# Six places of a hand-ordered layer kernel: state copies ahead of a gate, weights ahead of halves, turns and sums later, most of the last norm's sums earlier

## The chip, the cores and the metric

One core of a Trainium2 chip. The metric is device microseconds for one launch, the median of several runs. Names of engines: PE is TensorE's matmul, PEld its weight load (which overlaps matmuls), DVE is VectorE, ACT ScalarE, POOL GpSimd, SP the queue that issues loads.

## The reference, cut to what matters

One layer of a hybrid decoder at width 1024, for 320 tokens (256 of a prompt, 8 sequences of 8 tokens that continue old states), in float32:

```
x = x + 0.5 * g1 * swiglu(modulate(rmsnorm(x)))            # ff1
mq, mk, mv, mo, mi, mf, z, xbc, dtp, ga, gb = split(u @ w_in)
hm = mlstm(conv(mq, mk), mv, gates, C, n, m)               # 4 heads, 256 x 512 states
ya = (headnorm(hm) * sigmoid(mo)) @ w_pa
ys = ssd(conv(xbc), dt, A, h) + D * xs                     # 32 heads in 4 groups
gg = ys * silu(z)
gg = gg * rsqrt(mean(gg * gg over a group's 512) + EPS)    # group norm
yb = (gg * s_norm_g) @ w_pb
x = x + g2 * ((sigmoid(ga) * ya + sigmoid(gb) * yb) @ w_out)
x = x + 0.5 * g3 * swiglu(modulate(rmsnorm(x)))            # ff2
y = rmsnorm(x, final_norm)
```

## The kernel before

Activations lie transposed, 128 channels by 320 tokens a tile. Every product with a weight is cut into **units**: one unit gives one output tile of 128 channels from 8 weight tiles. Float32 accuracy comes from three products of halves: `dense` issues eight matmuls w_hi by u_hi, eight w_hi by u_lo, eight w_lo by u_hi, all into one of the banks of PSUM. ScalarE makes the high half of a unit's weights from the loaded ring (`high_ahead`, tile w_hi), VectorE the low half (`low_ahead`, tile w_lo), both two units ahead; the high half of the unit after next waits until the present unit is done, since there are two buffers.

Each engine has its own program, written by hand as loops over the same list of units; between the units it does the small work of that stage. What an engine does after which unit is given by `if i == ...` and by tables, so the order on each engine is fixed, and semaphores join them. The stages that matter here, in order:

- **The four mLSTM heads**, units v and mo. The last head has eight mo units (i = 0 to 7). `turn_head` transposes one of four 128-channel parts of a head's normalised output back; `TURN_SLOTS` says behind which unit. ScalarE normalises a head (`output_norm`, `hn_ready`); it gates with mo (`output_gate`), VectorE multiplies (`gated_head`) and splits.
- **pa**, then the first xbc units.
- **Four groups of the SSD** (`gr` 0 to 3), eight units each (`phase_units`). In the first three the fifth unit (i = 4) is an xbc unit, in the last it is a z unit. TensorE issues behind unit i: `decay_rows` (i < 4), `pack_inputs` (i = 2, waits for `hmask_ready`), `head_outputs(gr, i - 1)` (i = 1 to 4, waits for `w_ready`), in this order; `turn_states` and `sample_states` from i = 4. VectorE: `sample_masks` makes sample halves and masks (b_halves, x_halves, cm, `hmask_ready`) and the decays' rows; `weights` multiplies decays by scores (`w_ready`); `outputs` adds D * x. ScalarE: `old_states` copies turned states (`ht_read`), `gate` applies the gate's function to a bank.
- **Twelve tail units**: z 12 to 15, ga 4 to 7, gb 4 to 7 (i = 0 to 11). ScalarE squares a group's tiles, POOL adds the four tiles, TensorE sums over channels with one-column matmuls (`group_sums`, tile aux<-ones), ScalarE takes the roots of three groups at once (`roots(0, 3)`), VectorE their reciprocals (`group_roots` there, `rr_ready`), TensorE broadcasts them over partitions (`group_roots` there, aux<-ident,sm, behind unit i = 4), and VectorE scales the tiles (`group_norm`).
- **pb, out, ff2, the last norm**: seven tiles' squares are added by POOL while the eighth is computed; one-column matmuls sum both, then root, reciprocal, scaling and the store of y.

ScalarE's functions come in table sets; a change of set is an ACT_TABLE_LOAD in the profile. Copy and Square need no load of their own here.

Of the kernel before, what the change touches and what calls it, by code (L numbers as in the profile page):

```python
# [14 lines left out]
KD = D // 128  # L15
# [41 lines left out]
STEP_SLOTS = (1, 2, 4, 5)  # L57
TURN_SLOTS = ({}, {3: 0, 4: 1, 5: 2}, {0: 3, 3: 4, 4: 5, 5: 6}, {0: 7, 3: 8, 4: 9, 5: 10, 6: 11})
EARLY = {name: [(name, 0), (name, 1)] for name in ("qk", "up2")}
# [188 lines left out]
def build(nc, io, out):  # L248
# [5 lines left out]
    with ctx:  # L254
# [749 lines left out]
        def _(pe):  # L1004
# [805 lines left out]
            for i, u in enumerate(tail_units()):  # L1810
                dense(u)
                if i == 0:
                    turn_old_part(SG - 1)
                    pe.wait_ge(S["up_done"], 16)
                    turn_tails(4, 6, (banks[2], banks[3]))
                if i == 2:
                    group_sums(0)
                if i == 3:
                    group_sums(1)
                    group_sums(2)  # L1820
                if i == 4:
                    for gr in range(3):
                        group_roots(gr)
                if i == 6:
                    group_sums(3)
# [33 lines left out]
            pe.wait_ge(S["sq_summed"], 4 + SG)  # L1859
            pe.wait_ge(S["sq_ready"], 4 * KD)  # L1860
            for c in range(3):
                rows = 128 if c < 2 else 64
                t = slice(c * 128, c * 128 + rows)
                mm(aux[3][0:rows, c:c + 1], sq[:, 0, t], ones[:, 0:1], True, False)
                ins = mm(aux[3][0:rows, c:c + 1], sq[:, KD - 1, t], ones[:, 0:1], False, True)
            ins.then_inc(S["rowsum_done"], 1)
# [4 lines left out]
        def _(act):  # L1871
# [517 lines left out]
            for gr in range(SG):  # L2389
                us = phase_units(gr)  # L2390
                for i, u in enumerate(us):
                    if i >= 5:
                        old_states(gr, i - 4)
                    high_ahead(u)
                    if u.name == "xbc":
                        conv(u, pad2, 3)
                    elif u.name == "gb":
                        if u.own == 0:
                            act.wait_ge(S["conv_silu"], 40)
                        kept_gate(u, ACT.Copy)  # L2400
                    else:
                        gate(u, ACT.Copy if i < 4 else gate_func(u))
# [21 lines left out]
                    if i == 5:  # L2424
                        act.wait_ge(S["ph_mm"], gr + 1)
                        copy(prompt_h, aux[2][:, :]).then_inc(S["ph_copied"], 1)
                    if i == 4:
                        old_states(gr, 0)
# [28 lines left out]
            for i, u in enumerate(tail_units()):  # L2457
# [9 lines left out]
                if i == 1:  # L2467
                    squares(2)
                if i == 3:
                    roots(0, 3)  # L2470
                if i == 4:
                    squares(3)
                    nc.scalar.activation(merged_g[:, 0:4, :], merged_g[:, 0:4, :], ACT.Sigmoid).then_inc(S["gate_open"], 1)
                    for r in range(4):
                        act.wait_ge(state_out[r], 16 * old_uses[r] + 32 * SG)
                    act.wait_ge(prompt_sent, 16 * (MH + SG))
# [52 lines left out]
        def _(dve):  # L2529
# [722 lines left out]
            for gr in range(SG):  # L3252
                for i, u in enumerate(phase_units(gr)):
# [12 lines left out]
                    if i == 0:  # L3266
                        group_rows(gr)
                        masked_scores(gr)
                    if i == 1:
                        if gr > 0:  # L3270
                            old_part(gr - 1)
                        sample_masks(gr)
                    if i < 4 and not amid:
                        weights(gr, i)
                    if 1 <= i <= 3 and not amid:
                        outputs(gr, i - 1)
                    if i == 4:
                        weighted_inputs(gr)
# [27 lines left out]
            for i, u in enumerate(tail_units()):  # L3306
# [3 lines left out]
                if u.name != "gb":  # L3310
                    gated(u, ya if u.name == "ga" else xbc_t)
                if i == 3:
                    group_roots(0, 3)
# [93 lines left out]
```

## Time and profile before

| | |
|---|---|
| median of 3 runs | 1263.19 us (1263.02 to 1265.1) |
| profiled execution | 1262.8 us |
| its span, first to last instruction | 1261.1 us |
| mean granted TensorE clock | 0.993 |
| PE busy | 1240.4 us, 98% |
| PEld busy | 1144.7 us, 91% |
| DVE, ACT, POOL busy | 783.3, 620.8, 220.8 us |
| HBM | 190 GB/s over the span |

The span is what the trace covers; the profiled execution's own time is 1.7 us more. A busy PE is not PE at its peak, since the ends of matmuls are modelled; idle TensorE shows in the timelines as a bracket behind a row, with the length of the idle time and what ended it. The table's shares are averages over all stages; the places of the change are looked at one by one below.

### The profile page before, as it was taken

To read this page: it belongs to the slowest core of one execution; us is meant where nothing else is said; L and a number is where in the kernel's file an instruction comes from. 1 tells how busy PE (TensorE), PEld (TensorE's weight loads), DVE (VectorE), ACT (ScalarE), POOL (GpSimd) and SP (SyncE) were. 2 spreads that over 40 slices of the span, in tenths; PEclk is the share of its full clock that TensorE was granted. 3 is DMA by queue.
4 is the path that set the end of the run, shared out by engine and by line. 5 is a ranking of instruction groups with operands and counts; after the bars stand their busy time and mean duration, and the time that the engine had idled before them with its cause. 6 is when DMAs were issued, how large, how long until landed. Compare 5 with 4: busy or idle time off the path is not lost. (4 is left out here: it accounts for less than half of the span.)

```text
span 1261.1 us, 22606 instructions
## 1 busy us (share of the span) xinstructions
PE 1240.4 (98%) x9059; PEld 1144.7 (91%) x9059; DVE 783.3 (62%) x1345; ACT 620.8 (49%) x1102; POOL 220.8 (18%) x385
## 2 busy tenths in 40 slices
PE   8999999999999999999999999999999999999997
PEld 5999989998988777779999989989999999999997
DVE  4744444547976667675388787875676885455432
ACT  5523324335668555655356776565543453333432
POOL 5100000012640212130033333414200300000000
PEclk8999999999999999999999999999999999999998
DMA  9998879553324788986474558365454454653541
GB/s 310 264 345 261 260 252 300 158 167 127 117 85 145 254 299 306 355 272 173 140 206 129 158 153 243 105 206 155 127 138 152 152 190 145 200 160 111 161 138 42
DMA packets 258629, 241.54 MB, mean 192 GB/s; under 512 B 8205, under 2 KB 242141, under 8 KB 258526
## 3 DMA queue, kind: packets, MB, share of 16 engines
q1 hardware_dynamic: 249850, 211.16, 54.6%
q0 software_dynamic: 8576, 28.91, 6.8%
q8 instruction: 72, 1.18, 0.4%
q14 instruction: 31, 0.25, 0.1%
q10 hardware_dynamic: 100, 0.04, 0.0%
HBM read 209.88 MB, written 30.21 MB: 190 GB/s over the span
## 5 line engine op out<-in xcount | busy, mean ns | idle before, releaser
L2552 DVE TENSOR_TENSOR w_lo<-ring,w_hi 128x1024 fp32r<-128x1024 f32 (+1 forms) x264 | 337.6, 1279 | 354.4 <-ACT w_hi L1889 353.8
L1889 ACT ACTIVATE w_hi<-ring 128x1024 fp32r<-128x1024 f32 (+1 forms) x264 | 289.6, 1097 | 485.7 <-PE bank L1010 441.7
L1010 PE MATMUL bank<-u_hi,w_hi 128*128 128x320 f32 x1472 | 257.5, 316 | 0.7 <-ACT w_hi L1889 0.5
L1010 PE MATMUL bank<-u_hi,w_lo 128*128 128x320 f32 x1472 | 247.0, 310 | 0.4 <-DVE w_lo L2552 0.4
L1010 PE MATMUL bank<-u_lo,w_hi 128*128 128x320 f32 x1472 | 246.4, 310 | 0.0
L1010 PEld LDWEIGHTS bank<-u_hi,w_hi 128*128 128x128 f32 x1472 | 222.8, 188 | 16.3 <-issue 9.6
L1010 PEld LDWEIGHTS bank<-u_hi,w_lo 128*128 128x128 f32 x1472 | 223.7, 188 | 1.3 <-DVE w_lo L2552 1.2
L1010 PEld LDWEIGHTS bank<-u_lo,w_hi 128*128 128x128 f32 x1472 | 224.3, 188 | 0.1
L818 POOL TENSOR_TENSOR arena<-x_t,gain 128x64 f32<-128x64 f32 x16 | 4.8, 298 | 337.4 <-DVE x_t L2634 337.4
L1010 PE MATMUL bank<-ff_hi,w_hi 128*128 128x320 f32 x352 | 57.5, 310 | 0.0
L1010 PE MATMUL bank<-ff_hi,w_lo 128*128 128x320 f32 x352 | 56.8, 308 | 0.0
L1010 PE MATMUL bank<-ff_lo,w_hi 128*128 128x320 f32 x352 | 56.8, 308 | 0.0
L1010 PEld LDWEIGHTS bank<-ff_hi,w_hi 128*128 128x128 f32 x352 | 52.7, 188 | 0.4 <-issue 0.4
L1010 PEld LDWEIGHTS bank<-ff_hi,w_lo 128*128 128x128 f32 x352 | 52.9, 188 | 0.0
L1010 PEld LDWEIGHTS bank<-ff_lo,w_hi 128*128 128x128 f32 x352 | 52.9, 188 | 0.0
L1007 PE MATMUL aux<-ident,arena 128*128 128x128 f32 (+4 forms) x325 | 49.7, 278 | 3.0 <-ACT arena L1875 1.6
L790 POOL TENSOR_TENSOR arena<-arena 128x320 f32<-128x320 f32 x12 | 10.4, 868 | 226.0 <-ACT arena L1908 225.2
L2822 DVE SCALAR_TENSOR_TENSOR arena<-arena,par 128x344 f32<-128x344 f32 x80 | 46.7, 584 | 3.9 <-POOL arena L858 1.8
L1010 PE MATMUL bank<-y_hi,w_hi 128*128 128x320 f32 x272 | 45.9, 310 | 0.0
L1007 PEld LDWEIGHTS aux<-ident,arena 128*128 128x128 f32 (+4 forms) x325 | 37.2, 141 | 9.5 <-issue 4.3
L1010 PE MATMUL bank<-y_hi,w_lo 128*128 128x320 f32 x272 | 45.8, 310 | 0.0
L1010 PE MATMUL bank<-y_lo,w_hi 128*128 128x320 f32 x272 | 45.7, 309 | 0.0
(426 smaller groups left out, 1682.1 us busy)
## 6 DMA issues: line engine op xcount, KB each, us to landing
ring<-in_w_in SPq DMA_DIRECT2D x52, 1024.0 KB, 5.4
ring<-in_ff_w SPq DMA_DIRECT2D x44, 1024.0 KB, 7.5
ring<-in_ff_w SPq DMA_DIRECT2D x32, 704.0 KB, 4.7
arena<-in_ada_w SPq DMA_DIRECT2D x20, 1024.0 KB, 10.0
ring<-in_ada_w SPq DMA_DIRECT2D x16, 1024.0 KB, 11.9
arena<-in_state_mlstm_C SPq DMA_DIRECT2D x22, 512.0 KB, 6.6
out_s_C<-arena POOLq DMA_DIRECT2D x22, 512.0 KB, 6.9
ring<-in_w_pa SPq DMA_DIRECT2D x8, 1024.0 KB, 8.0
```

The lines of the kernel that those rows point to most:

```text
L790: ins = nc.gpsimd.tensor_tensor(sq[:, 0, :], sq[:, 0, :], sq[:, kc, :], ALU.add)
L818: nc.gpsimd.tensor_tensor(sequences(xg_s[n][:, kc, :]), sequences(x_t[:, kc, TP:T]), gain[:, kc, 1:NSEQ].unsqueeze(2).to_broadcast([128, S ...
L1007: return nc.tensor.transpose(dst, src, ident[0:rows, 0:rows])
L1010: return nc.tensor.matmul(dst, lhs, rhs, start=first, stop=last)
L1889: nc.scalar.activation(w_hi[v.split_no % 2][:, 0:v.kc, :], panel_part(v), ACT.Copy).then_inc(S["hi_done"], 1)
L2552: V.tensor_tensor(w_lo[r][:, 0:v.kc, :], panel_part(v), w_hi[r][:, 0:v.kc, :].bitcast(FP32), ALU.subtract)\
L2822: ch.link(V.scalar_tensor_tensor(out=a, in0=p[:, tap:tap + CONVW], scalar=par[:, c + w_col + tap * tiles:c + w_col + tap * tiles + 1], in1 ...
```

## The change

Six edits of order; no arithmetic is changed, and no instruction added or removed but for one table load on ScalarE.

1. ScalarE, last group: the copies of the first turned states stand ahead of the fifth unit's gate, not behind.
2. VectorE, every group, behind the second unit: `weights` and `outputs` stand ahead of `sample_masks`.
3. Last head: four of its five turns move one slot later (3, 4, 5, 6 to 4, 5, 6, 7). The table is read by TensorE, ScalarE (`gated_high`) and VectorE (`gated_head`, `gated_low`).
4. TensorE, tail: the third group's sums move from behind the fourth unit into the fifth, between its first and second eight matmuls.
5. ScalarE and VectorE, tail: the roots of three groups and their reciprocals move from behind the fourth unit's gate to behind the fifth's. TensorE's broadcasts of them stay behind the fifth unit.
6. TensorE, last norm: for each block of tokens the sum over seven tiles and the eighth's square stood together, behind the wait for the latter; now the three of the seven tiles come first, then the wait, then the three of the eighth. Only the first of the six starts an accumulation.

```diff
--- before.py
+++ after.py
@@ -55,7 +55,7 @@
 PA_ORDER = (0, 2, 4, 6, 1, 3, 5, 7) + tuple(range(8, 16))
 PART_ORDER = (0, 2, 4, 1, 3, 5) + tuple(range(6, 16))
 STEP_SLOTS = (1, 2, 4, 5)
-TURN_SLOTS = ({}, {3: 0, 4: 1, 5: 2}, {0: 3, 3: 4, 4: 5, 5: 6}, {0: 7, 3: 8, 4: 9, 5: 10, 6: 11})
+TURN_SLOTS = ({}, {3: 0, 4: 1, 5: 2}, {0: 3, 3: 4, 4: 5, 5: 6}, {0: 7, 4: 8, 5: 9, 6: 10, 7: 11})
 EARLY = {name: [(name, 0), (name, 1)] for name in ("qk", "up2")}
 CONV_AT = {0: (), 1: (), 2: (0,), 3: (1,), 4: (2,), 5: (3, 4), 6: (5,), 7: (6, 7)}
 XBC_FIRST = tuple(range(16, 24)) + tuple(range(4))
@@ -1808,7 +1808,7 @@
 
             pe.wait_ge(S["tails_saved"], 40)
             for i, u in enumerate(tail_units()):
-                dense(u)
+                dense(u, inner=(lambda: group_sums(2)) if i == 4 else None)
                 if i == 0:
                     turn_old_part(SG - 1)
                     pe.wait_ge(S["up_done"], 16)
@@ -1817,7 +1817,6 @@
                     group_sums(0)
                 if i == 3:
                     group_sums(1)
-                    group_sums(2)
                 if i == 4:
                     for gr in range(3):
                         group_roots(gr)
@@ -1857,12 +1856,13 @@
                 if u.closes and u.own > 0:
                     turn_result(u.own - 1)
             pe.wait_ge(S["sq_summed"], 4 + SG)
-            pe.wait_ge(S["sq_ready"], 4 * KD)
-            for c in range(3):
-                rows = 128 if c < 2 else 64
-                t = slice(c * 128, c * 128 + rows)
-                mm(aux[3][0:rows, c:c + 1], sq[:, 0, t], ones[:, 0:1], True, False)
-                ins = mm(aux[3][0:rows, c:c + 1], sq[:, KD - 1, t], ones[:, 0:1], False, True)
+            for kc in (0, KD - 1):
+                if kc > 0:
+                    pe.wait_ge(S["sq_ready"], 4 * KD)
+                for c in (0, 2, 1):
+                    rows = 128 if c < 2 else 64
+                    t = slice(c * 128, c * 128 + rows)
+                    ins = mm(aux[3][0:rows, c:c + 1], sq[:, kc, t], ones[:, 0:1], kc == 0 and c == 0, kc > 0 and c == 1)
             ins.then_inc(S["rowsum_done"], 1)
             turn_result(KD - 1)
 
@@ -2392,6 +2392,8 @@
                     if i >= 5:
                         old_states(gr, i - 4)
                     high_ahead(u)
+                    if i == 4 and u.name != "xbc":
+                        old_states(gr, 0)
                     if u.name == "xbc":
                         conv(u, pad2, 3)
                     elif u.name == "gb":
@@ -2424,7 +2426,7 @@
                     if i == 5:
                         act.wait_ge(S["ph_mm"], gr + 1)
                         copy(prompt_h, aux[2][:, :]).then_inc(S["ph_copied"], 1)
-                    if i == 4:
+                    if i == 4 and u.name == "xbc":
                         old_states(gr, 0)
                     if i == 7:
                         old_part(gr)
@@ -2466,9 +2468,8 @@
                     squares(1)
                 if i == 1:
                     squares(2)
-                if i == 3:
+                if i == 4:
                     roots(0, 3)
-                if i == 4:
                     squares(3)
                     nc.scalar.activation(merged_g[:, 0:4, :], merged_g[:, 0:4, :], ACT.Sigmoid).then_inc(S["gate_open"], 1)
                     for r in range(4):
@@ -3266,14 +3267,14 @@
                     if i == 0:
                         group_rows(gr)
                         masked_scores(gr)
-                    if i == 1:
-                        if gr > 0:
-                            old_part(gr - 1)
-                        sample_masks(gr)
+                    if i == 1 and gr > 0:
+                        old_part(gr - 1)
                     if i < 4 and not amid:
                         weights(gr, i)
                     if 1 <= i <= 3 and not amid:
                         outputs(gr, i - 1)
+                    if i == 1:
+                        sample_masks(gr)
                     if i == 4:
                         weighted_inputs(gr)
                         if u.name == "xbc":
@@ -3309,7 +3310,7 @@
                     old_part(SG - 1)
                 if u.name != "gb":
                     gated(u, ya if u.name == "ga" else xbc_t)
-                if i == 3:
+                if i == 4:
                     group_roots(0, 3)
                 if 4 <= i <= 9:
                     for c in range(2 * (i - 4), 2 * (i - 4) + 2):
```

How this moves instructions, at three places. First ScalarE in the tail, from the copy behind the fourth unit on; arena<-bank is a gate, sm<-aux,eps_col the roots of the three groups, w_hi<-ring a high half, arena<-arena 128x1280 a square (and, last, the sigmoid of the merge gates). Before:

```order
L1889 ACTIVATE w_hi<-ring 128x1024
L2314 ACTIVATE arena<-bank 128x320
L2449 ACT_TABLE_LOAD
L2449 ACTIVATE sm<-aux,eps_col 128x2x3
L2450 ACTIVATE sm<-aux,eps_col 64x3
L1889 ACTIVATE w_hi<-ring 128x1024
L2314 ACT_TABLE_LOAD
L2314 ACTIVATE arena<-bank 128x320
L2443 ACTIVATE arena<-arena 128x1280
L2473 ACTIVATE arena<-arena 128x1280
```

The same place in the changed kernel (its lines are two further on):

```order
L1889 ACTIVATE w_hi<-ring 128x1024
L2314 ACTIVATE arena<-bank 128x320
L1889 ACTIVATE w_hi<-ring 128x1024
L2314 ACT_TABLE_LOAD
L2314 ACTIVATE arena<-bank 128x320
L2451 ACT_TABLE_LOAD
L2451 ACTIVATE sm<-aux,eps_col 128x2x3
L2452 ACTIVATE sm<-aux,eps_col 64x3
L2445 ACTIVATE arena<-arena 128x1280
L2474 ACT_TABLE_LOAD
L2474 ACTIVATE arena<-arena 128x1280
```

The roots moved behind the next unit's high half, table load and gate, and a further table load stands ahead of the last sigmoid.

TensorE at the same place: the one-column sums of the second and third group (two rows each), and the unit around them; the broadcasts follow the unit's last eight matmuls in both kernels.

```order
 L1010 MATMUL aux<-ones,arena 128x1 x2
 L1010 MATMUL aux<-ones,arena 64x1
+L1010 MATMUL bank<-u_hi,w_hi 128x320 x8
 L1010 MATMUL aux<-ones,arena 128x1 x2
 L1010 MATMUL aux<-ones,arena 64x1
-L1010 MATMUL bank<-u_hi,w_hi 128x320 x8
 L1010 MATMUL bank<-u_lo,w_hi 128x320 x8
 L1010 MATMUL bank<-u_hi,w_lo 128x320 x8
```

The first eight matmuls of the unit moved ahead of the third group's sums.

VectorE in a group, behind the second unit: weights is the 128x896 row, outputs the 128x320 row, the four rows from b_halves on are `sample_masks`. Before:

```order
L3249 TENSOR_TENSOR arena<-arena 128x2x4x32
L3187 TENSOR_TENSOR b_halves<-arena,b_halves 64x128
L3188 TENSOR_TENSOR x_halves<-arena,x_halves 64x512
L3190 TENSOR_TENSOR arena<-arena,seg_b 128x128 x2
L3195 TENSOR_TENSOR w_lo_rest<-sm,tile_of_head 32x256
L3216 SCALAR_TENSOR_TENSOR arena<-arena 128x896
L3221 SCALAR_TENSOR_TENSOR arena<-arena,h_dec,bank 128x320
```

And in the changed kernel (its lines are one further on):

```order
L3250 TENSOR_TENSOR arena<-arena 128x2x4x32
L3217 SCALAR_TENSOR_TENSOR arena<-arena 128x896
L3222 SCALAR_TENSOR_TENSOR arena<-arena,h_dec,bank 128x320
L3188 TENSOR_TENSOR b_halves<-arena,b_halves 64x128
L3189 TENSOR_TENSOR x_halves<-arena,x_halves 64x512
L3191 TENSOR_TENSOR arena<-arena,seg_b 128x128 x2
L3196 TENSOR_TENSOR w_lo_rest<-sm,tile_of_head 32x256
```

Weights and outputs moved ahead of the halves, the masks and the decays' rows.

## Rows read from the trace of the kernel before

**Rows 1.** The page: busy time, share and instructions of each engine.

```profile
PE 1240.4 (98%) x9059; PEld 1144.7 (91%) x9059; DVE 783.3 (62%) x1345; ACT 620.8 (49%) x1102; POOL 220.8 (18%) x385
```

**Rows 2.** Windows: stretch, length, PE busy, granted clock, DMA share, GB/s.

```profile
11.70:18.50 6.80, 6.80 (x44) 0.50 1.10 350
...
888.90:892.30 3.40, 3.40 (x15) 0.50 0.76 216
```

**Rows 3.** Timelines: start, us, engine, line; PE in two groups, ACT in the last.

```profile
749.42 0.66 PE L1010 MATMUL bank<-pack_b,pack_x 32*128 32x128 f32 x8
750.02 1.09 PE L1007 MATMUL aux<-ident,arena 128*128 128x128 f32 x8
...
848.76 0.66 PE L1010 MATMUL bank<-pack_b,pack_x 32*128 32x128 f32 x8
850.43 1.06 PE L1007 MATMUL aux<-ident,arena 128*128 128x128 f32 x8 [1.01 <-ACT arena L1875]
...
848.06 1.28 ACT L2314 ACT_TABLE_LOAD   x1
```

**Rows 4.** Timelines of ACT, DVE and PEld, second group, second and third unit.

```profile
733.30 0.35 ACT L2371 ACTIVATE arena<-aux,g 128x64 f32<-128x64 f32 x1
...
733.30 0.42 DVE L3249 TENSOR_TENSOR arena<-arena 128x256 f32<-128x256 f32 x1
734.23 0.28 DVE L3187 TENSOR_TENSOR b_halves<-arena,b_halves 64x128 fp32r<-64x128 f32 x1 [0.51 <-ACT x_halves L1875]
...
735.15 0.49 DVE L3190 TENSOR_TENSOR arena<-arena,seg_b 128x128 f32<-128x128 f32 x2
...
735.89 1.07 DVE L3216 SCALAR_TENSOR_TENSOR arena<-arena 128x896 f32<-128x896 f32 x1
736.89 0.53 DVE L3221 SCALAR_TENSOR_TENSOR arena<-arena,h_dec,bank 128x320 f32<-128x320 f32 x1
...
735.87 0.39 PEld L1010 LDWEIGHTS aux<-x_halves,pick_x 128*128 128x128 f32 x2
737.02 0.63 PEld L1010 LDWEIGHTS bank<-arena 128*64 128x64 f32 x8 [0.75 <-DVE arena L3216]
```

**Rows 5.** Timelines of PEld, ACT and PE around the last head.

```profile
545.93 0.31 PEld L1007 LDWEIGHTS bank<-ident,arena 128*128 128x128 f32 x3 [0.94 <-ACT arena L2265]
...
573.44 0.80 ACT L2265 ACTIVATE arena<-arena,coef 64x512 f32<-64x512 f32 x1
...
575.24 1.47 PE L1007 MATMUL aux<-ident,arena 128*128 128x128 f32 x12
```

**Rows 6.** Timelines of PEld, ACT and DVE in the tail units.

```profile
887.40 0.73 PEld L1010 LDWEIGHTS aux<-ones,arena 128*128 128x128 f32 x6 [0.82 <-POOL arena L986]
888.15 1.47 PEld L1010 LDWEIGHTS bank<-u_hi,w_hi 128*128 128x128 f32 x8
...
893.16 2.98 PEld L1010 LDWEIGHTS aux<-ident,sm 128*128 128x128 f32 x18
896.20 1.17 PEld L1010 LDWEIGHTS bank<-u_hi,w_hi 128*128 128x128 f32 x8
...
888.92 0.27 ACT L2449 ACTIVATE sm<-aux,eps_col 128x6 f32<-128x6 f32 x1
...
893.56 1.06 ACT L1889 ACTIVATE w_hi<-ring 128x1024 fp32r<-128x1024 f32 x1 [4.23 <-PE bank L1010]
894.64 1.28 ACT L2314 ACT_TABLE_LOAD   x1
895.93 0.44 ACT L2314 ACTIVATE arena<-bank 128x320 f32<-128x320 f32 x1
...
889.47 0.12 DVE L3294 RECIPROCAL sm<-sm 64x3 f32<-64x3 f32 x1
```

**Rows 7.** Timeline of PE at the end of the program.

```profile
1252.29 1.35 PE L1010 MATMUL aux<-ones,arena 128*128 128x1 f32 x12 [1.30 <-ACT arena L1908]
1253.57 0.55 PE L1007 MATMUL aux<-ident,arena 128*128 128x128 f32 x3
```

## The prediction

> **What bounds the kernel now.** The page first: TensorE is busy for 1240.4 of 1261.1 us [rows 1], and no other engine for more than 62%. So only time in which TensorE waits, or runs slowly, can be won or lost, and whatever it loses lasts to the end. The timelines of its matmuls (PE) and weight loads (PEld) show where it stands still at the places that the diff touches; there the other engines' timelines say what ends last. The windows show where its clock is not at full: two stretches only, 6.8 us at the start and 3.4 us from 888.9, both at half rate, 1.2 of 2.4 GHz [rows 2]. Between the waits a unit of 24 matmuls takes 3 x 1.17 = 3.5 us [rows 6].
>
> **State copies ahead of the gate (a gain of 1.05).** The edit acts in the last group alone, whose fifth unit is a z unit. Now ScalarE loads a table (1.28) and copies the gate before the two state copies, and TensorE's turns of the next states wait 1.01 for them: from the packed products to these turns it is 1.67 us, against 0.60 in the second group, where no table load stands there [rows 3]. With the copies first, nothing new is waited for: 1.67 - 0.60 = 1.07, taken as 1.05. The gate comes some 1.1 us later; the bank that it frees is opened two units on, over 7 us away, so I cost that at nothing. Without the cover it would be 1.1.
>
> **Weights ahead of halves (a loss of 0.7, four places).** In a group's second unit VectorE makes the sample halves and masks (from 734.23), then the rows for the grown decays, then weights (735.89, 1.07), and TensorE waits 0.75 for these [rows 4]. It looks like a gain of 0.5: the packing's two matmuls of 512 columns stream for 0.43 at 2.4 GHz behind a load of some 0.2, so to about 736.5, and from there to 737.02 nothing streams. But TensorE's own order is inputs packed, then outputs, and packing needs the masks, which now come last. After: the weights can start when VectorE's addition ends, 733.30 + 0.42 = 733.72, and ScalarE's last exponential is done (733.65); with 0.03 for the start, 733.75. Weights to outputs take 1.00, the outputs 0.53 less the same overlap of 0.07, halves to masks 0.92, the masks 0.49: done at 736.62, seen by TensorE at 736.68 (weights ended at 736.96 and TensorE went on at 737.02). The packing that started at 735.87 now waits 0.81, and behind it lie its 0.43, with or without the 0.2: outputs start at 737.1 to 737.3, against 737.02 [rows 4]. That is +0.1 to +0.3 a group; I take nearly 0.2, so 0.7, with 0.3 to 1.2 for the four. The first group lacks the addition but has the same order and nearly the same waits.
>
> **A head's turns one slot later (a gain of 0.9).** The turn in slot 3 of the last head waits 0.94 for the normalised rows [rows 5]. One slot later they are long there. The turn itself moves behind the last mo unit and costs the same there. Late next could be the last head's own rows: they are ready at 573.44 + 0.80 = 574.24 and asked for at 575.24 [rows 5], 1.0 of slack. TensorE comes 0.9 sooner, and ScalarE too, less one gated copy that now lies ahead (about 0.4): some 0.5 of slack is left, and if it is used up the gain shrinks by as much. Bounds: 0.94 and 0.5.
>
> **Last norm's sums ahead (a gain of 0.65).** Twelve passes of one column take 1253.57 - 1252.29 = 1.28, behind a wait of 1.30 for the last square, and everything behind them waits [rows 7]. Six go into that wait. Half of 1.28 is 0.64. Bounds: 0.5 and 0.7.
>
> **A group's sums later, and the roots.** Three terms.
> The wait for the third group's sums, 0.82 [rows 6], goes: eight matmuls of the next unit (1.17) now lie ahead of them. -0.8.
> Behind it stands the low clock. That unit takes 893.16 - 888.15 = 5.01 instead of 3.51, since from 888.9 the granted clock is 0.50 [rows 2, 6]. Ahead of the fall there were twelve one-column passes and the wait; with 1.2 us of dense matmuls between them and no wait I expect no fall. -1.5.
> But the square roots now come behind the fifth unit's gate on ScalarE, and the gate needs the fifth unit finished; TensorE's broadcasts of the roots still stand right behind that unit, and wait for them. Now that unit covers the roots; the cover goes. The chain, from the unit's last load (893.16 now): 0.40 to the copy of high halves, 2.37 from there to the gate (1.06 copy, 1.29 table load), 0.44 gate, 1.29 for a second table load, 0.67 from the first root to the end of the reciprocals (888.92 to 889.47 + 0.12), 0.05 to be seen. Sum 5.22 [rows 6]. TensorE has nothing else queued ahead of the broadcasts: +5.2. VectorE's normalisation of tiles stands behind the reciprocals; its results are first needed by pb, seven units on.
> The clock falls in such a wait, by what a far shorter one did [rows 2]. The 18 broadcast passes then run slower: 0.166 each now, while twelve turns of 128 columns take 0.12 each at full rate [rows 5], so 0.24 at half, and 18 x 0.075 = 1.3 at most. What is left of the slow stretch lies on dense matmuls. Bounds: nothing, and 1.3 + 1.5 with dense matmuls slowed as at 888.9. I take 0.8, since much of such a stretch passes in the wait itself.
> The three and the clock: -0.8 - 1.5 + 5.2 + 0.8 = +3.7. The further table load that the sigmoid of the merge gates now needs (1.28) lies under the next unit.
>
> A rule speaks against this even more. The Trainium skill, ScalarE: Activation LUTs, section What ACT_TABLE_LOAD costs, puts 1.38 us of drain beside the 1.28 of each switch. This trace disagrees: the high copy ends at 894.62 and the load begins at 894.64, and the gate begins as the load ends [rows 6]. By the page the chain would be longer by 2 x 1.38, and the sum +4.5.
>
> **Sum.** -1.05 + 0.7 - 0.9 - 0.65 + 3.7 = +1.8. The profiled execution took 1262.8 (span 1261.1 and 1.7 around it), the median is 1263.19; both shift alike: 1265.0 us. It is 0.14%, and a measurement of this kernel tells 0.2% (2.5 us) from no change: under 1260.7 is faster, over 1265.7 slower.
>
> **The rivals.**
> As summed: the wait for the roots eats the gains. Adding the bounds that are likely together gives 1263.6 to 1266.9. 0.63.
> The clock stays low longer, as in the 6.8 us at the start [rows 2], slower. Place: behind the roots' wait. Price: 4.3 us of slowed broadcasts (+1.3) and 2.5 of dense matmuls at half rate (+1.2), 2.5 instead of 0.8: 1266.7. It decides once the slow clock costs over 1.5 there (0.8, and the 0.7 up to 1265.7). For it: such a stretch exists, with light work in it; against: the later one lasted only 3.4. 0.16. The Trainium skill, TensorE: Matmul & The Clock Gate, Part 1, says that the default of the array's clock is throttled and activity releases it. The trace agrees in so far as both stretches began in light work and ended in activity; between their lengths no row decides.
> The weights do win: if packing were not waited for, 4 x 0.5 = 2.0 is gained instead of 0.7 lost: 1262.3, no change. For it: the wait is named for the weights. Against: packing needs the masks, and the sum of VectorE's work ahead of it grows by 1.46. 0.08.
> The roots' wait is not what it seems, and the change is faster: if the broadcasts found the roots ready, 5.2 + 0.8 would go: 1259.0. For it: everything else in the change gains. Against: their chain starts at the end of the very unit that they follow. 0.06.
> Table loads with their drain: by a wait longer by 2.8 us, 1267.8. Against it, the rows' gap of 0.02. 0.07.
>
> **How the numbers follow.** 1265.0 is the likeliest case's. Its own range, 1263.6 to 1266.9, widened towards both neighbours until 2 in 10 is out, is 1262.3 to 1267.4. Slower: 0.16 + 0.07 and the upper sixth of the first case, 0.12, is 0.35. Faster: 0.06, and 0.02 of the third. Same: 0.57.
>
> **What would show it.** In the profile after: the broadcasts of the roots (aux<-ident,sm) preceded by some 5 us of idle TensorE, and a granted clock of 0.50 there; no idle before the third group's sums, and a full clock in the unit around them; the packing (x_halves,pick_x) waiting 0.8 in each group for masks, and the outputs behind it for nothing; no wait before the turns of states in the last group, nor before the last head's first late turn; six one-column passes before the last square, six after. If the wait for the roots is under 3 us, the forecast is wrong and the kernel faster; if the outputs in the groups start earlier than now, the second step is wrong.

## The result and the profile after

The changed kernel takes 1273.6 us (median of 4 runs, 1272.98 to 1273.89) against 1263.51 beside it: ratio 1.0077, interval 1.006 to 1.0094. It is slower by 10.1 us, where 1.8 was forecast, and lies above the range. Its profiled execution took 1272.98 us, with a span of 1270.0 against 1261.1.

The page's first part after; it answers to [rows 1]. PE's busy time has grown by 5.0 us though no matmul was added. Not all of that is the change's: up to a row of the last head just ahead of the first edit's place (540.27 before, 540.83 after) PE is busy 534.05 us against 531.86, and stands still 1.6 less. From there to the end it is busy 2.8 us more and stands still 5.5 more.

```profile
PE 1245.4 (98%) x9059; PEld 1147.1 (90%) x9059; DVE 783.7 (62%) x1345; ACT 622.7 (49%) x1103; POOL 217.4 (17%) x385
```

**A new wait at the last head.** First the timeline of PEld after, from the last rows of the last head into pa; then ACT's and DVE's of the same stretch (start, us, engine and line; in the bracket the idle time before and what ended it). They answer to [rows 5].

```profile
573.18 1.18 PEld L1010 LDWEIGHTS bank<-y_hi,w_hi 128*128 128x128 f32 x8 [1.89 <-issue]
...
578.31 1.29 PEld L1007 LDWEIGHTS aux<-ident,arena 128*128 128x128 f32 x12 [1.61 <-ACT arena L2265]
```

```profile
568.13 0.59 ACT L1875 ACTIVATE arena<-bank 64x512 f32<-64x512 f32 x1 [4.99 <-PE bank L1007]
...
572.67 0.44 ACT L2188 ACTIVATE arena<-bank 128x320 f32<-128x320 f32 x1 [1.95 <-DVE w_lo_rest L3040]
...
577.46 0.80 ACT L2265 ACTIVATE arena<-arena,coef 64x512 f32<-64x512 f32 x1
```

```profile
568.76 0.68 DVE L3049 TENSOR_TENSOR arena<-bank,arena 64x512 f32<-64x512 f32 x1 [4.62 <-ACT arena L1875]
...
571.92 0.17 DVE L3061 TENSOR_SCALAR coef<-coef 128x3 f32<-128x3 f32 x1
572.03 0.55 DVE L3040 SCALAR_TENSOR_TENSOR w_lo_rest<-bank,par,arena 128x320 f32<-128x320 f32 x1
```

The wait of 0.94 in slot 3 is gone, but two waits, 1.89 and 1.61, have come. Read them backwards. pa's second unit starts 0.07 after ScalarE's gate (572.67 + 0.44) frees its bank. The gate waited 1.95 for VectorE's product with the twelfth turn (572.03), and that product stands behind the statistics of the last head's rows (568.76 to 572.09). These began late since ScalarE stood idle for 4.99 us ahead of the copy of those rows (568.13), until a TensorE transposition had been done. In the code that copy is `output_rows(3)`, which overwrites the tile nm that the turns read, so it waits until all twelve turns are done (`hn_turned`), and the twelfth now comes behind the last mo unit. Before, the same copy waited for nothing; ACT's row:

```profile
563.80 0.59 ACT L1875 ACTIVATE arena<-bank 64x512 f32<-64x512 f32 x1
```

The norm of the rows, which ended at 574.24 before, ends at 578.26, and the turns of pa wait for it.

**The packing waits for the masks.** The timelines of PEld and DVE in the second group; they answer to [rows 4].

```profile
740.38 0.30 PEld L1010 LDWEIGHTS aux<-x_halves,pick_x 128*128 128x128 f32 x2 [0.95 <-DVE arena L3191]
741.04 0.63 PEld L1010 LDWEIGHTS bank<-arena 128*64 128x64 f32 x8 [0.37 <-issue]
```

```profile
738.34 0.54 DVE L3222 SCALAR_TENSOR_TENSOR arena<-arena,h_dec,bank 128x320 f32<-128x320 f32 x1
738.91 0.28 DVE L3188 TENSOR_TENSOR b_halves<-arena,b_halves 64x128 fp32r<-64x128 f32 x1
...
739.83 0.49 DVE L3191 TENSOR_TENSOR arena<-arena,seg_b 128x128 f32<-128x128 f32 x2
```

The packing waits 0.95 for VectorE's masks, and the outputs start 0.66 behind it: 1.61 where before it was 737.02 - 735.87 = 1.15 [rows 4]. That is +0.46 in this group. By the same two rows it is 0.44, 0.47 and 0.47 in the other three, 1.8 in all.

**The roots.** PEld in the tail, then ACT, then the windows with the granted clock (stretch, length, busy times, clock, DMA share, GB/s); they answer to [rows 6] and [rows 2].

```profile
893.53 1.22 PEld L1010 LDWEIGHTS bank<-u_hi,w_lo 128*128 128x128 f32 x8
899.96 0.74 PEld L1010 LDWEIGHTS aux<-ident,sm 128*128 128x128 f32 x4 [5.21 <-DVE sm L3295]
...
905.07 2.05 PEld L1010 LDWEIGHTS bank<-u_hi,w_hi 128*128 128x128 f32 x8
...
909.41 1.22 PEld L1010 LDWEIGHTS bank<-u_hi,w_hi 128*128 128x128 f32 x8
```

```profile
895.11 1.06 ACT L1889 ACTIVATE w_hi<-ring 128x1024 fp32r<-128x1024 f32 x1 [3.61 <-PE bank L1010]
896.18 1.28 ACT L2314 ACT_TABLE_LOAD   x1
897.48 0.44 ACT L2314 ACTIVATE arena<-bank 128x320 f32<-128x320 f32 x1
897.93 1.28 ACT L2451 ACT_TABLE_LOAD   x1
899.23 0.27 ACT L2451 ACTIVATE sm<-aux,eps_col 128x6 f32<-128x6 f32 x1
```

```profile
888.50:900.20 11.70, 6.76 (x49) 6.43 (x48) 5.60 (x8) 6.41 (x9) 2.67 (x2) 1.00 0.44 127
900.20:907.00 6.80, 6.80 (x25) 5.77 (x25) 1.01 (x2) 3.15 (x3) 2.39 (x2) 0.50 0.00 0
```

The wait is the forecast one, 5.21. The clock is full all through it and falls to 1.2 GHz only 0.2 us after work has begun again. So the whole slow stretch lies on work: the 18 broadcasts take 905.07 - 899.96 = 5.11 against 3.04, the next unit 909.41 - 905.07 = 4.34 against 3.48: 2.9 us.

The other steps went as forecast. The sums of the third group wait for nothing, and the unit around them runs at full clock. In the last group the turns of the next states come 0.59 behind the packed products, against 1.67 [rows 3]; PE after:

```profile
853.70 0.66 PE L1010 MATMUL bank<-pack_b,pack_x 32*128 32x128 f32 x8
854.29 1.09 PE L1007 MATMUL aux<-ident,arena 128*128 128x128 f32 x8
```

PEld at the end of the program, which answers to [rows 7]:

```profile
1260.11 0.36 PEld L1007 LDWEIGHTS aux<-ident,arena 128*128 128x128 f32 x3
1260.47 0.82 PEld L1010 LDWEIGHTS aux<-ones,arena 128*128 128x128 f32 x6
1261.95 0.81 PEld L1010 LDWEIGHTS aux<-ones,arena 128*128 128x128 f32 x6 [0.66 <-ACT arena L1908]
1262.60 0.37 PEld L1007 LDWEIGHTS aux<-ident,arena 128*128 128x128 f32 x3
```

And the same two turns before:

```profile
1250.35 0.37 PEld L1007 LDWEIGHTS aux<-ident,arena 128*128 128x128 f32 x3
...
1253.56 0.28 PEld L1007 LDWEIGHTS aux<-ident,arena 128*128 128x128 f32 x3
```

From one turn to the next it is 2.49 after and was 3.21 before, a gain of 0.72.

### The profile page after: what moved, and what is told of

Read it like the earlier page. It is cut to its first block and busy times, and to the rows that moved or that the text cites. A ratio compares the mean times of both kernels' runs of the same rounds, so it can differ in the third digit from the quotient of the medians.

```text
span 1270.0 us, 22609 instructions
## 1 busy us (share of the span) xinstructions
PE 1245.4 (98%) x9059; PEld 1147.1 (90%) x9059; DVE 783.7 (62%) x1345; ACT 622.7 (49%) x1103; POOL 217.4 (17%) x385
## 5 line engine op out<-in xcount | busy, mean ns | idle before, releaser
L790 POOL TENSOR_TENSOR arena<-arena 128x320 f32<-128x320 f32 x12 | 10.4, 867 | 226.5 <-ACT arena L1908 225.2
```

Of the source, the lines that this page charges most:

```text
L790: ins = nc.gpsimd.tensor_tensor(sq[:, 0, :], sq[:, 0, :], sq[:, kc, :], ALU.add)
```

## The experiments

All are made from the kernel before. The start of the program varies by some 4 us between executions of any of these kernels, so beside the medians I give a distance inside each profiled execution: from a row of TensorE in the last head (aux<-vp,kpm x2 with an idle time of 0.84, at 540.27 before) to the turn behind the last norm's sums (1253.57 before, the last row of [rows 7]). It leaves the start out, but it is one execution of each kernel and has no interval. A last column says whether the clock fell in or behind the third group's sums, ahead of the broadcasts, as it did before ([rows 2], worth 1.5).

| kernel | median us | before beside it | ratio and interval | distance, us | less before's | fall at the sums |
|---|---|---|---|---|---|---|
| before | 1263.19 | | | 713.30 | | yes |
| after | 1273.6 | 1263.51 | 1.0077 [1.006, 1.0094] | 721.88 | +8.6 | no |
| roots_only | 1273.2 | 1264.0 | 1.0076 [1.006, 1.0092] | 720.68 | +7.4 | no |
| turns_only | 1266.51 | 1264.0 | 1.002 [1.0011, 1.0029] | 716.02 | +2.7 | yes |
| masks_only | 1265.64 | 1264.0 | 1.0016 [1.0006, 1.0026] | 715.11 | +1.8 | yes |
| copies_and_last_sums | 1262.59 | 1264.0 | 0.9989 [0.9978, 1.0] | 710.26 | -3.0 | no |
| last_turn_only | 1268.39 | 1263.67 | 1.004 [1.0026, 1.0054] | 716.84 | +3.5 | yes |
| turns_two | 1262.22 | 1263.67 | 0.9992 [0.9982, 1.0001] | 711.00 | -2.3 | no |
| sums_in_unit_roots_kept | 1262.69 | 1263.67 | 0.9991 [0.9982, 1.0] | 711.11 | -2.2 | no |
| roots_before_gate | 1268.6 | 1263.67 | 1.0043 [1.0029, 1.0056] | 719.08 | +5.8 | no |
| roots_only_spun | 1267.04 | 1263.26 | 1.0023 [1.0014, 1.0033] | 716.18 | +2.9 | no |
| weights_then_masks | 1263.19 | 1263.26 | 1.0003 [0.9994, 1.0012] | 711.84 | -1.5 | no |
| masks_split | 1262.24 | 1263.26 | 0.9991 [0.9981, 1.0] | 711.94 | -1.4 | yes |
| best | 1257.1 | 1263.26 | 0.9949 [0.9936, 0.9962] | 707.05 | -6.3 | no |

### Parts of the change, alone

**roots_only**: the third group's sums into the fifth unit, and roots and reciprocals behind its gate (edits 4 and 5).

```diff
-                dense(u)
+                dense(u, inner=(lambda: group_sums(2)) if i == 4 else None)
...
-                if i == 3:
+                if i == 4:
                     roots(0, 3)
```

> Only the third group's sums move into the fifth tail unit and the roots behind its gate. Theory: a wait of 5.2 us before the broadcasts, and behind it a stretch of 6.8 us at half clock that lies wholly on work, +2.9 us; less the 2.3 gained before, +5.9 us. Rival, as predicted: +3.7 us, half clock costing 0.8.

**turns_only**: edit 3 alone.

```diff
-TURN_SLOTS = (..., {0: 7, 3: 8, 4: 9, 5: 10, 6: 11})
+TURN_SLOTS = (..., {0: 7, 4: 8, 5: 9, 6: 10, 7: 11})
```

> Only the last head's turns move one slot later. Theory: ScalarE's copy of the last head's numerators waits until the twelfth turn has been issued (it overwrites the rows that the turns read); that turn now stands behind the last mo unit, so the copy, the statistics and the norm come some 4 us later and TensorE waits for them in pa, 1.9 and 1.6 us: +2.6 us in all, after the 0.9 gained in slot 3. Rival, the step as I predicted it: -0.9 us, and the 3.5 lost in pa come from another part of the change.

**masks_only**: edit 2 alone, `sample_masks` behind weights and outputs.

```diff
-                        sample_masks(gr)
                     if i < 4 and not amid:
                         weights(gr, i)
                     if 1 <= i <= 3 and not amid:
                         outputs(gr, i - 1)
+                    if i == 1:
+                        sample_masks(gr)
```

> Only VectorE's weights and outputs move ahead of halves and masks. Theory: +0.45 us in each of four groups, +1.8 us: the packing waits 0.9 for the masks, and the outputs behind it start 0.66 after the packing does. Rival, as predicted: +0.7 us, the packing waiting 0.8 and the outputs following after 0.43 to 0.63.

**copies_and_last_sums**: edits 1 and 6.

```diff
+                    if i == 4 and u.name != "xbc":
+                        old_states(gr, 0)
...
+            for kc in (0, KD - 1):
+                if kc > 0:
+                    pe.wait_ge(S["sq_ready"], 4 * KD)
```

> Only the state copies ahead of the last group's gate, and the last norm's sums of seven tiles ahead of the eighth's square. As predicted: -1.05 - 0.65 = -1.7 us, 1261.5. If the four parts add up (2.6 + 1.8 + 5.9 - 1.7 = 8.6), no part acts on another. Rival: the sum of the four differs from the whole by over 1 us, and parts act on each other.

Measured: the roots are the largest loss, and turns and masks lose as well. The last two edits gain; of their 3.0, 1.5 is the fall of the clock that did not come in this execution. The four medians add up to 9.2 + 2.5 + 1.6 - 1.4 = 11.9 against 10.1 for the whole. In the distances, without the 1.5, they give 7.4 + 2.7 + 1.8 - 1.5 = 10.4 against 8.6. Of these 1.8, 1.4 are explained: in roots_only's execution the slow stretch was longer. The other 0.4 is left open. PEld of roots_only, and the windows:

```profile
900.23 0.93 PEld L1010 LDWEIGHTS aux<-ident,sm 128*128 128x128 f32 x4 [5.21 <-DVE sm L3292]
...
905.53 2.10 PEld L1010 LDWEIGHTS bank<-u_hi,w_hi 128*128 128x128 f32 x8
...
911.07 1.22 PEld L1010 LDWEIGHTS bank<-u_hi,w_hi 128*128 128x128 f32 x8
```

```profile
900.30:910.30 10.00, 10.00 (x36) 8.97 (x37) 1.00 (x2) 3.32 (x3) 2.40 (x2) 0.51 0.00 0
```

The same wait of 5.21, then 5.30 for the broadcasts and 5.54 for the unit, 4.3 us more than at full clock (2.26 and 2.06), where it was 2.9 after.

### Which turn does the harm

**last_turn_only**: only the twelfth turn moves, from slot 6 to 7.

```diff
+TURN_SLOTS = (..., {0: 7, 3: 8, 4: 9, 5: 10, 7: 11})
```

> Only the twelfth turn moves, from slot 6 to slot 7 of the last head; turns 8 to 10 stand as before. Theory (ScalarE's copy of the last head's rows waits for the twelfth turn, and holds the high copy and the gate behind it): TensorE waits some 1.9 us ahead of pa's second unit and some 1.6 us ahead of the turns of pa, as where all four turns are late, and the wait of 0.94 us in slot 3 is back too: +3.5 us of TensorE time around the last head, about 1266.7. Rival (what hurts is that all four turns lie one slot later, so that each delays ScalarE's chain a little): the two waits are under 1 us together, and the time is within 0.5 us of before.

**turns_two**: the other three move one slot, and the twelfth shares slot 6 with the eleventh.

```diff
+TURN_SLOTS = (..., {0: 7, 4: 8, 5: 9, 6: 10})
...
+                        turn_head(2, 3)
...
+                        gated_high(11)
```

> Turns 8, 9 and 10 one slot later (slots 4, 5 and 6), but the twelfth turn stays in slot 6, behind the eleventh; nothing stands behind the last mo unit. Theory (the twelfth turn's place behind the last mo unit is the whole harm): the wait of 0.94 us in slot 3 is gone, the waits of 1.9 and 1.6 us of the changed kernel are gone, and TensorE gains 0.9 us: about 1262.5. Rival (a later place for any turn delays the last head's rows): waits of over 0.5 us stay ahead of the turns of pa, and nothing is gained.

Timeline of PEld, last_turn_only:

```profile
546.74 0.31 PEld L1007 LDWEIGHTS bank<-ident,arena 128*128 128x128 f32 x3 [0.94 <-ACT arena L2265]
...
574.32 1.19 PEld L1010 LDWEIGHTS bank<-y_hi,w_hi 128*128 128x128 f32 x8 [1.89 <-issue]
...
579.45 1.29 PEld L1007 LDWEIGHTS aux<-ident,arena 128*128 128x128 f32 x12 [1.59 <-ACT arena L2265]
```

And PEld, then ACT, of turns_two:

```profile
576.13 1.38 PEld L1007 LDWEIGHTS aux<-ident,arena 128*128 128x128 f32 x12
```

```profile
565.99 0.59 ACT L1876 ACTIVATE arena<-bank 64x512 f32<-64x512 f32 x1 [1.47 <-PE bank L1007]
...
574.48 0.80 ACT L2266 ACTIVATE arena<-arena,coef 64x512 f32<-64x512 f32 x1
```

The twelfth turn alone brings both waits, and the old 0.94 with them: the distance is 3.5 longer, as the theory says. The median moved by 4.7, 1.2 more than the distance, and why is open. With it in slot 6 the copy of the last head's rows waits 1.47, the norm ends at 575.28, and nothing waits. The distance is 2.3 shorter, 1.5 of it the absent fall and 0.9 the wait that is gone. By medians the gain can't be told from none.

### The roots: wait and clock apart

**sums_in_unit_roots_kept**: edit 4 without edit 5.

```diff
+                dense(u, inner=(lambda: group_sums(2)) if i == 4 else None)
```

> The third group's sums inside the fifth tail unit, while ScalarE's roots stay behind the fourth unit's gate. Theory (the loss of this part is the roots' place alone): no wait of 0.82 us ahead of the sums; the broadcasts of the roots wait for nothing; the clock stays full from 885 to 910 us: -0.8, and a further -1.5 where the kernel before has its slow clock there: 1261.2 to 1262.7. Rival (sums later make the roots late as well): the roots wait for the sums, whose end is now 1.2 us later, and the broadcasts wait 0.5 to 1.5 us: no gain.

**roots_before_gate**: behind the fifth unit's high half but ahead of its gate; the reciprocals ahead of the product with the gate.

```diff
+                if i == 4:
+                    roots(0, 3)
...
-                if i == 3:
-                    roots(0, 3)
```

> The third group's sums inside the fifth tail unit; the roots behind ScalarE's high half of the fifth unit but ahead of its gate, the reciprocals ahead of VectorE's product with the gate. Theory (the broadcasts wait for the chain on ScalarE behind the fifth unit): high copy, table load, roots, reciprocals remain, the gate and its table load fall out: the wait is 3.4 us instead of 5.2, and a slow stretch of the clock still follows; +2.6 for the wait less the 0.8 of the sums and up to 2.9 for the clock: 1266 to 1270. Rival (what slows TensorE is the broadcasts' own work of narrow passes, not the wait): the slow stretch is as long as with the wait of 5.2 us.

**roots_only_spun**: as roots_only, with 22 products of the identity with itself ahead of the broadcasts; the result goes to a bank that nobody reads.

```diff
+                    pe.wait_ge(S["tail_cp"], 2)
+                    spin(22)
```

> As with the roots behind the fifth unit's gate, but TensorE multiplies the identity by itself 22 times ahead of the broadcasts (work that computes nothing and whose result nobody reads), so that it is busy in the time in which it waits for the roots. Theory (the roots' chain costs 5.2 us, and the idle wait itself brings the slow clock, which costs 2.9 us and more behind it): the broadcasts start as late as without the added work, the granted clock stays full, they take 3.0 us and the next unit 3.5: 2.9 to 4 us less than the kernel with the roots moved alone, about 1269.5. Rival (the slow clock comes from the narrow passes of the broadcasts): the clock falls there as before and nothing is won; also if the added work lasts past the roots, the broadcasts come later by that.

PEld of sums_in_unit_roots_kept, then of roots_before_gate, then of roots_only_spun:

```profile
889.16 0.76 PEld L1010 LDWEIGHTS aux<-ones,arena 128*128 128x128 f32 x6
...
892.24 2.98 PEld L1010 LDWEIGHTS aux<-ident,sm 128*128 128x128 f32 x18
```

```profile
895.84 0.93 PEld L1010 LDWEIGHTS aux<-ident,sm 128*128 128x128 f32 x4 [3.46 <-DVE sm L3293]
...
901.14 2.10 PEld L1010 LDWEIGHTS bank<-u_hi,w_hi 128*128 128x128 f32 x8
...
906.82 1.22 PEld L1010 LDWEIGHTS bank<-u_hi,w_hi 128*128 128x128 f32 x8
```

```profile
891.90 5.03 PEld L1010 LDWEIGHTS bank<-ident 128*128 128x128 f32 x44
897.16 2.94 PEld L1010 LDWEIGHTS aux<-ident,sm 128*128 128x128 f32 x18 [0.23 <-DVE sm L3294]
900.16 1.17 PEld L1010 LDWEIGHTS bank<-u_hi,w_hi 128*128 128x128 f32 x8
...
903.64 1.22 PEld L1010 LDWEIGHTS bank<-u_hi,w_hi 128*128 128x128 f32 x8
```

With the roots where they were, neither wait nor slow clock is there: edit 4 by itself shortens the distance by 2.2 (the median by 1.0, hardly clear of none), edit 5 does the harm. With the roots ahead of the gate the wait is 3.46, as worked out, and the distance is still 5.8 longer (the median 4.9). The broadcasts take 5.30 and the unit 5.68, so a wait shorter by a third did not bring a cheaper slow stretch than 5.21 did. With the wait filled by useless work, the broadcasts start 897.16 - 891.90 = 5.26 behind the unit's last load, as late as with idle time; but the clock stays full, the broadcasts take 3.00 and the unit 3.48. The distance is 4.5 less than roots_only's, and the median lies 3.8 above before instead of 9.2. That settles it for this place: idle time ahead of the broadcasts, not their narrow passes, brings the slow clock. The full clock was seen in one profiled execution, and the median of nine runs agrees. The distances add up: 5.26 - 0.82 - 1.5 = +2.9 for the spun kernel (+2.9 measured), and 4.3 more, +7.2, for roots_only (+7.4 measured).

### The order of masks and weights

**weights_then_masks**: weights, masks, outputs.

```diff
                     if i < 4 and not amid:
                         weights(gr, i)
+                    if i == 1:
+                        sample_masks(gr)
                     if 1 <= i <= 3 and not amid:
                         outputs(gr, i - 1)
```

> VectorE's second unit of a group in the order weights, masks, outputs (before: masks, weights, outputs; the changed kernel: weights, outputs, masks). Theory (the packing waits for the masks, and the outputs behind it for the later of packing and weights): the masks come 0.53 us sooner than in the changed kernel, the packing waits 0.3 to 0.5 us, and the outputs start 0 to 0.2 us sooner a group than before: 0 to -0.8 us in all, against +1.8 with the masks last. Rival (whatever stands ahead of the masks costs as much as it lasts): +0.3 a group or more, 1265 or more.

**masks_split**: the masks cm, then the halves, weights and outputs, and the grown decays' rows last, in a function of their own.

```diff
+            def grown_input(gr):
...
+                    if i == 1:
+                        grown_input(gr)
```

> The masks first, then the halves that the packing needs, then weights, outputs, and the rows of the grown decays last (before: these rows ahead of the weights). Theory (TensorE needs first the masks and halves and then the weights, and the rows of the grown decays late): the packing waits for nothing and the wait for the weights, 0.75 us in a group, shrinks by the time of what no longer lies ahead of them, 0.3 to 0.5 us: -1.2 to -2.0 in four groups, about 1262. Rival (ScalarE's exponentials, not VectorE's queue, hold the weights): the wait stays and the time is that of before.

PEld of weights_then_masks and of masks_split in the second group:

```profile
738.21 0.30 PEld L1010 LDWEIGHTS aux<-x_halves,pick_x 128*128 128x128 f32 x2 [0.48 <-DVE arena L3190]
738.88 0.63 PEld L1010 LDWEIGHTS bank<-arena 128*64 128x64 f32 x8 [0.36 <-issue]
```

```profile
736.73 0.39 PEld L1010 LDWEIGHTS aux<-x_halves,pick_x 128*128 128x128 f32 x2
737.49 0.63 PEld L1010 LDWEIGHTS bank<-arena 128*64 128x64 f32 x8 [0.36 <-DVE arena L3216]
```

In the first the packing waits 0.48, against 0.95 with the masks last, and from there to the outputs it is 0.67: 1.15 together, what it was before: no gain, no loss, and the 1.5 in its distance is the absent fall. In the second the packing waits for nothing, and the outputs come 0.76 behind it instead of 1.15, 0.39 sooner. Over the four groups (0.33 in the first, 0.38 to 0.39 in the others) that is 1.5, and the distance, in an execution that did have the fall, is 1.4 shorter. By medians it is 1.0, just at the edge of its interval. VectorE's queue held the weights, not the exponentials: the last of these had ended at 733.65 before, and the weights began at 735.89 [rows 4].

### All gains together

**best**: edits 1, 4 and 6, turns_two and masks_split.

> All that should gain, together: the state copies ahead of the last group's gate and the last norm's sums of seven tiles ahead of the last square, as in the change; the third group's sums inside the fifth tail unit with the roots where they were before; turns 8 to 10 one slot later and the twelfth in slot 6; the split order of masks and weights. Theory: -1.05 - 0.65 - 0.8 - 0.9 and -1.2 to -2.0, and -1.5 more in executions in which the clock would have fallen behind the sums: -4.6 to -6.9, so 1257 to 1259.5. Rival (a gain upstream is given back at the next wait, a DMA or ScalarE): less than half of it shows.

1257.1 us, 6.2 under before beside it, and 16.5 under the changed kernel's median. The distance is 6.25 shorter, the terms give 1.08 + 0.72 + 0.82 + 0.93 + 1.5 + 1.5 = 6.55. Each gain passed to the end nearly whole.

## Why the prediction was wrong, step by step

- **State copies ahead of the gate** (-1.05): right, 1.67 to 0.59, with nothing waiting for the later gate. Measured together with the last norm's sums, which gained 0.72 for 0.65: the pair's distance is 1.5 shorter beside the clock's 1.5, 0.3 less than the two rows give; the median is 1.4 lower, for 1.7 forecast.
- **Weights ahead of halves** (+0.7): right mechanism, size off by a factor of over two; it is +1.8, above the bound of 1.2. Two terms were short. The packing waits 0.95, not 0.81, mostly since the halves start 0.57 behind the outputs and not 0.46. And the outputs follow the packing by 0.66, where the prediction had 0.43 to 0.63 and, with 0.7 for four places, took 0.52. Each adds 0.14 a group, 1.1 in all.
- **A head's turns one slot later** (-0.9): this step failed. "The turn itself moves behind the last mo unit and costs the same there" looked at TensorE's cost and not at who waits for the turn. "TensorE comes 0.9 sooner, and ScalarE too" was the opposite of what happened for ScalarE: its copy of the rows went from 563.80 to 568.13, since it waits for the twelfth turn. It is 1.89 + 1.61 - 0.94 = +2.6 instead of -0.9. The wait was to be seen in the code (a copy that overwrites the tile that the turns read) and not in the trace of before, where the twelfth turn was done by 562.03 (the turns' weights are loaded at 561.63, for 0.40) and the copy had no idle time.
- **The group's sums and the roots** (+3.7): the wait of 0.82 and the fall of 1.5 went, and the chain of 5.22 came, to the hundredth (5.21). The half clock failed as a size: 0.8 taken, 2.9 measured after, and 4.3 and 4.5 in two other kernels' executions, above the bound of 2.8. I took the low value, "since much of such a stretch passes in the wait itself". Hardly any of it does: the fall comes within 0.4 us of the moment at which work resumes. The rival of the longer stretch had the length right (6.8, in that execution) and priced it at 2.5 with 1.3 for the broadcasts, which took 2.1 more; a pass of theirs takes 0.284 (5.11 / 18) against 0.169, not 0.24. Its time, 1266.7, still missed, since it kept the forecast for turns and masks. The reading that the clock is low in two stretches only missed a third, from 1254.0 to the end of the trace of before. It begins 0.4 behind the start of TensorE's last turn, so it cost next to nothing there.
- **Table loads without drain**: right; loads follow the activation before them by 0.01 to 0.02 and take 1.28. The Trainium skill (ScalarE: Activation LUTs, What ACT_TABLE_LOAD costs) has 1.38 of drain for each switch. This trace doesn't agree: with two of them the wait would have been 8.0 by estimate, and it was 5.21.
- **Sum.** The roots and sums come to 5.21 - 0.82 - 1.5 + 2.9 = 5.8 for 3.7, turns and masks to +2.6 and +1.8 for -0.9 and +0.7, and 1.8 goes off for the copies and the last sums: 8.4, of 8.6 measured in the distance. The turns are 3.5 of the error of nearly 7, the clock 2.1, the masks 1.1. The median moved 1.5 more than the distance. For the profiled executions the rest can be read: their times are 10.2 apart (1272.98 and 1262.8), of which 8.6 is the distance, 0.6 the start, -0.2 the stretch behind the last turn, and 1.3 time outside the span (3.0 against 1.7), whose cause is open. For the medians the length of the slow stretch, which differs between executions, may count as well; that is not shown.

## What to carry to other kernels

Before a step is moved later, list every wait on its semaphore and every write over what it reads: a wait that costs nothing in the trace of before has no row there, and it is the one that opens. A chain whose cover is taken away costs its length, and where TensorE stands idle for it, price the slow clock behind it by its full stretch, laid on the work that follows, unless something fills the wait. Sort a queue by who is asked first, with finer pieces than the functions of the code: the masks ahead of the weights and the unneeded rows behind both gained, while each order of whole functions lost or changed nothing.

## What the runs showed of the hardware

- Behind waits of 3.46 to 5.21 us of TensorE the granted clock was full for nearly all of the wait and fell to 1.2 GHz about when work began, in all three profiled executions that had one: 0.2 us after it in the changed kernel, at the same time in roots_before_gate, 0.35 before it in roots_only. In windows of 0.1 us the stretches lasted 6.8, 10.2 and 10.2 us. The same wait of 5.21 had one of 6.8 and one of 10.2, so the length of the wait did not set that of the stretch. Waits of 1.89 and 1.61 at the last head had no fall behind them, in three executions.
- A wait of 0.82 between six one-column passes and the next six was followed by some 3.4 us at half clock in five of the eight profiled executions that had it (before among them), and by none in three, with the same instructions at that place. With the sums inside a unit, no execution of six had it. So part of the gain of such an edit (1.5) depends on the execution.
- The Trainium skill (TensorE: Matmul & The Clock Gate, Part 1) says that activity releases the throttled clock. The runs agree in part: 44 small passes (22 float32 products of 128 columns) over 5.03 us kept the clock full where idle time lost it. Activity alone did not end a stretch soon: in roots_only it went on through 5.30 us of broadcasts and most of the unit behind them.
- The start varies: the row at 540.27 before lies between 540.27 and 544.28 in fourteen executions, and 3.3 of the 3.6 us by which copies_and_last_sums is late have already gathered at its first products of states, at 72.75 against 69.44. Why they gather there was not tried by experiment. The half clock at the start differs too: three executions had no such stretch in the first 34 us, the others one or two of 3.4 to 7.0 us, and a short start does not go with its absence (540.27 before, with 7.0 us of it; 540.64 in turns_only, with none). A distance inside one execution can show changes under 2 us that medians of ten runs leave open, if chance falls of the clock are looked for and counted apart.
